# Latent attention on one core: ScalarE takes the exponential of the next unit before the copies of this unit's turned pieces

## The chip, the cores and the metric

One NeuronCore of a Trainium2 chip runs the whole layer. The metric is the device time of one execution in microseconds (us). The profile is of one execution of the same program. The engines are TensorE (PE; PEld is its weight load), VectorE (DVE), ScalarE (ACT), GpSimd (POOL) and SyncE (SP). Each engine runs its instructions in the order in which they are written for it, and waits for the others only at semaphores.

## The reference, cut to what matters

The layer is a hybrid decoder block on 1024 tokens of width 1024: latent attention (MLA) beside a chunkwise retention, then cross-attention to 256 memory tokens, then a gated convolution-MLP. The change touches the causal softmax attention of the eight MLA heads, with 64 + 32 query and key columns and 64 value columns:

```python
s = jnp.einsum('bhqd,bhkd->bhqk', q_blk, k).astype(jnp.float32) * scale
s = jnp.where(kpos[None, :] <= qpos[:, None], s, neg)
p = jax.nn.softmax(s, axis=-1).astype(v.dtype)
return jnp.einsum('bhqk,bhkd->bhqd', p, v)
```

Every product of the kernel is made of three matmuls, since each operand is held as a high and a low part (the high part is a rounded copy, the low part is the full value less the copy).

## The kernel before

Latent attention is worked in 64 **units**, eight for each of eight heads. A unit is a block of 128 queries, number i, with the keys of the blocks 0 to i, so it has (i + 1) x 128 columns. Within a head the blocks come in the order 1, 3, 2, 0, 5, 7, 6, 4 (`QORDER`). This text calls the places of a head r0 to r7, so r0 has 256 columns, r1 512, r2 384, r3 128, r4 768, r5 1024, r6 896 and r7 640. Units r0 to r3 have one **piece** of up to 512 columns, r4 to r7 have two.

What a unit w goes through:

- PE `m_scores(w)` (L824): the scores into PSUM banks 2 and 3, or 4 and 5. They are written two units ahead of the turning.
- DVE `m_max(w)` (L2138): the row maximum (L2143) and its negative times the scale (L2146), which raises `m_neg`.
- ACT `m_exp(w)` (L1444): it waits for `m_neg` and writes the exponentials of the whole row into `prow` (L1449), with the row sum.
- PE `m_turn(w)` (L845): it waits for `m_exp`, then transposes `prow` 128 columns at a time (L852) into bank 6 or 7, which the pieces take by turns. Piece q waits until the low part of piece q - 2 has been taken.
- ACT `m_pth(w)` (L1452): a rounded copy of each turned piece (`p0h` or `p1h`, the high part; the line shown by the profile is the helper's, L1178).
- DVE `m_ptl(w)` (L2149): the low part of each piece (`p0l` or `p1l`, L1829), which sets the bank free.
- PE `m_pv(g)` (L856): after four units (a half head) the products with the values (L873), 12 matmuls for the first half of a head and 24 for the second, then `ainv` turned into bank 0 (L886). ACT `m_sum(g)` copies that (`oT`), DVE `m_out(g)` multiplies (L2171).
- `aux(h + 1, n)`: in the units r2, r3, r4 and r6 PE makes a part of the next head's keys or queries in bank 0 (L547, L552, L553, or L818); ACT `aux_hi` copies it (`kbh`, `mqh`), DVE `aux_lo` takes the low part (`kbl`, `mql`). In the last head there is none; the output's high and low parts (`oth`, `otl`) are made there instead.

The order of each engine is written out by hand in a loop over the units, with nothing that reorders it. In iteration w the engines have:

- PE: `m_turn(w)`, `aux`, `m_scores(w + 2)`, and where w is a multiple of four `m_pv(w // 4 - 1)`.
- ACT: `m_sum` (where w % 4 is 1), `m_pth(w)`, `m_exp(w + 1)`, `aux_hi`.
- DVE: `m_out` (where w % 4 is 1), `m_ptl(w)`, `aux_lo`, `m_max(w + 2)`, then the reciprocal of the row sum, `m_inv(w + 1)` (L2162).

After the loop come the turning of x, the mixing product, and the rest of the layer, nearly all of it bound by PE. SP and POOL prepare weights for later stages meanwhile (`raw`, `wh`, `over_rings`); only the four slabs for the mixing product wait for PE's last use of the slot in this stage (L818).

Of the kernel before, what the change touches and what calls it, by code (L numbers as in the profile page):

```python
# [135 lines left out]
def build(nc, x, mem, pos, slabs, small, const, out):  # L136
# [23 lines left out]
    with ctx:  # L160
# [1015 lines left out]
        def _(act):  # L1176
# [243 lines left out]
            def aux_hi(h, n):  # L1420
                act.wait_ge(S["aux_t"], USE_OF["aux", h, n] + 1)
                b = n % 2
                if n < 2:
                    copy(kbh[0:NOPE, h % 2, half(b)], ps[0:NOPE, 0, :]).then_inc(S["aux_hi"], 1)
                else:
                    copy(mqh[0:QK, b, :], ps[0:QK, 0, :]).then_inc(S["aux_hi"], 1)

            def m_sum(g):

                h, b = divmod(g, 2)  # L1430
                r = slice(h % 2 * DV, (h % 2 + 1) * DV)
                act.wait_ge(S["aux_t"], USE_OF["sum", g] + 1)
                copy(oT[r, h // 2, half(b)], ps[r, 0, :]).then_inc(S["aux_hi"], 1)

            def o_hi(fb, b):
                act.wait_ge(S["aux_lo"], USE_OF["sum", 4 * fb + 2 + b] + 1)
                copy(oth[:, fb, half(b)], oT[:, fb, half(b)]).then_inc(S["o_hi"], 1)

            def s2(w):

                c = 2 + 2 * (w % 2)
                return ps[:, c:c + 2, :].rearrange("p a n -> p (a n)")

            def m_exp(w):  # L1444
                n = (UNITS[w][1] + 1) * P
                act.wait_ge(S["m_neg"], w + 1)
                if w >= 2:
                    act.wait_ge(S["m_ptt"], PIECE0[w - 1])
                act.activation(prow[:, w % 2, 0:n], s2(w)[:, 0:n], ACT.Exp, scale=QK ** -0.5,  # L1449
                               bias=aneg[:, 0, w % 4:w % 4 + 1], accum_out=asum[:, 0, w % 4:w % 4 + 1]).then_inc(S["m_exp"], 1)  # L1450

            def m_pth(w):  # L1452
                i, g = UNITS[w][1], w // CH
                at_least(act, S["m_pv"], g - 1)
                for n in range(i // CH + 1):
                    q = PIECE0[w] + n
                    c0, c1 = CH * n, min(CH * (n + 1), i + 1)
                    act.wait_ge(S["m_ptt"], q + 1)
                    copy((p1h if g % 2 else p0h)[:, c0:c1, i % CH * P:(i % CH + 1) * P],
                         ps[:, 6 + q % 2, 0:(c1 - c0) * P].rearrange("p (a n) -> p a n", n=P)).then_inc(  # L1460
                        S["m_pth"], 1)
# [3 lines left out]
            NW = len(UNITS)  # L1465
            m_exp(0)
            for w in range(NW):
                h, r = divmod(w, NT)
                if w > CH and w % CH == 1:
                    m_sum(w // CH - 1)  # L1470
                m_pth(w)
                if w + 1 < NW:
                    m_exp(w + 1)
                if r in AUX_AT and h + 1 < MH:
                    aux_hi(h + 1, AUX_AT[r])
                if h == MH - 1 and r < 4:
                    o_hi(r // 2, r % 2)
                if h == MH - 1 and r >= 6:
                    o_hi(2, r - 6)
# [1099 lines left out]
```

## Time and profile before

| | before |
|---|---|
| median of 3 runs | 1975.4 us (1971.09 to 1976.38) |
| profiled execution, its own time | 1980.84 us |
| its span in the profile | 1979.0 us |
| PE busy | 1855.0 us, 94% |
| PEld busy | 1536.0 us, 78% |
| DVE busy | 967.8 us, 49% |
| ACT busy | 668.3 us, 34% |
| POOL busy | 947.1 us, 48% |

Busy shares are averages over stages with different limits. The latent attention runs from 648.8 us, its first exponential, to about 860 us.

### The profile page before, as it was taken

To read this page: it belongs to the slowest core of one execution; us is meant where nothing else is said; L and a number is where in the kernel's file an instruction comes from. 1 tells how busy PE (TensorE), PEld (TensorE's weight loads), DVE (VectorE), ACT (ScalarE), POOL (GpSimd) and SP (SyncE) were. 2 spreads that over 40 slices of the span, in tenths; PEclk is the share of its full clock that TensorE was granted. 3 is DMA by queue.
4 is the path that set the end of the run, shared out by engine and by line. 5 is a ranking of instruction groups with operands and counts; after the bars stand their busy time and mean duration, and the time that the engine had idled before them with its cause. 6 is when DMAs were issued, how large, how long until landed. Compare 5 with 4: busy or idle time off the path is not lost.

```text
span 1979.0 us, 25491 instructions
## 1 busy us (share of the span) xinstructions
PE 1855.0 (94%) x8924; PEld 1536.0 (78%) x8924; DVE 967.8 (49%) x1531; ACT 668.3 (34%) x1161; POOL 947.1 (48%) x519
## 2 busy tenths in 40 slices
PE   7999999999997888879999989989999999699998
PEld 6788888888875777767878878768888888588887
DVE  4345454000007666637344553767777778732212
ACT  6322223110013555541132322544444444422212
POOL 5743333456644775204533213377777777533330
PEclk9999999999998899989999999999999999899999
DMA  6511111223314885034221114233333333453312
GB/s 243 202 33 33 32 42 43 85 96 95 95 54 164 308 314 193 22 132 166 96 91 59 61 57 160 80 102 128 116 127 118 120 128 111 171 192 126 107 54 85
DMA packets 69339, 229.55 MB, mean 116 GB/s; under 512 B 6544, under 2 KB 16912, under 8 KB 65936
## 3 DMA queue, kind: packets, MB, share of 16 engines
q1 hardware_dynamic: 48720, 159.31, 24.6%
q10 hardware_dynamic: 20544, 69.21, 9.3%
q8 instruction: 50, 0.82, 0.2%
q14 instruction: 25, 0.20, 0.0%
HBM read 168.73 MB, written 59.77 MB: 115 GB/s over the span
## 4 chain that ended last, share of the span: by engine, by line
PE 60%; issue 13%; POOL 12%; DVE 8%; ACT 5%; DMA 2%; POOLq 0%; ACTq 0%; SPq 0%; DVEq 0%
PE ps L547 17%; PE ps L552 17%; PE ps L553 17%; POOL wl L476 8%; PE ps L873 3%; POOL zB L483 2%; ACT prow L1449 1%; PE ps L852 1%; PE ps L1165 1%; PE ps L1167 1%; PE ps L1166 1%; DVE p1l L1829 1%; DVE t L1832 1%; DMA raw<-in_slabs 1%; DVE amax L2143 1%
## 5 line engine op out<-in xcount | busy, mean ns | idle before, releaser
L444 POOL TENSOR_SCALAR wh<-raw 128x1024 fp32r<-128x1024 f32 x76 | 210.7, 2772 | 599.2 <-PE ps L547 555.0
L547 PE MATMUL ps<-uh,wh 128*128 128x512 f32 (+1 forms) x576 | 229.3, 398 | 2.4 <-POOL wl L446 2.4
L552 PE MATMUL ps<-ul,wh 128*128 128x512 f32 (+1 forms) x576 | 226.1, 393 | 0.0
L553 PE MATMUL ps<-uh,wl 128*128 128x512 f32 (+1 forms) x576 | 226.0, 392 | 0.0
L446 POOL TENSOR_TENSOR wl<-raw,wh 128x1024 fp32r<-128x1024 f32 x76 | 181.7, 2391 | 6.4
L476 POOL TENSOR_TENSOR wl<-raw,wh 128x512 fp32r<-128x512 f32 x88 | 140.1, 1611 | 34.3 <-ACT wh L1178 34.3
L523 POOL TENSOR_TENSOR wl<-raw,wh 128x1024 fp32r<-128x1024 f32 x28 | 71.4, 2551 | 141.1 <-ACT wh L1178 141.1
L1832 DVE SCALAR_TENSOR_TENSOR ya<-zA,sm,ya 128x512 f32<-128x512 f32 x88 | 94.2, 1071 | 88.6 <-ACT ya L1687 81.4
L1832 DVE SCALAR_TENSOR_TENSOR yb<-zB,sm,yb 128x512 f32<-128x512 f32 x88 | 128.6, 1461 | 15.8 <-ACT yb L1687 9.6
L463 POOL TENSOR_TENSOR over_rings<-over_rings 128x512 f32<-128x512 f32 x88 | 112.9, 1284 | 45.8 <-DMA over_rings<-in_slabs 40.6
L1178 ACT ACTIVATE wh<-raw 128x512 fp32r<-128x512 f32 (+1 forms) x124 | 90.5, 748 | 115.8 <-PE ps L547 78.8
L547 PEld LDWEIGHTS ps<-uh,wh 128*128 128x128 f32 (+1 forms) x576 | 108.3, 188 | 25.8 <-POOL wl L446 2.6
L547 PE MATMUL ps<-fah,wh 128*128 128x512 f32 x288 | 113.4, 394 | 14.9 <-DVE fal L1829 14.4
L553 PEld LDWEIGHTS ps<-uh,wl 128*128 128x128 f32 (+1 forms) x576 | 107.9, 187 | 25.0
L552 PEld LDWEIGHTS ps<-ul,wh 128*128 128x128 f32 (+1 forms) x576 | 108.1, 188 | 23.1
L552 PE MATMUL ps<-fal,wh 128*128 128x512 f32 x288 | 113.0, 392 | 0.0
L553 PE MATMUL ps<-fah,wl 128*128 128x512 f32 x288 | 112.9, 392 | 0.0
L476 POOL TENSOR_TENSOR wl<-ssm,wh 128x512 fp32r<-128x512 f32 x44 | 66.5, 1513 | 75.3 <-ACT wh L1178 75.3
L2059 DVE TENSOR_TENSOR mxr<-ps,sig 128x512 f32<-128x512 f32 x16 | 11.1, 692 | 177.9 <-PE ps L553 177.9
L1063 PE MATMUL ps<-f0h,wh 128*128 128x512 f32 x176 | 70.3, 400 | 8.6 <-DVE u L2371 4.2
L547 PEld LDWEIGHTS ps<-fah,wh 128*128 128x128 f32 x288 | 54.7, 190 | 27.0 <-DVE fal L1829 14.8
L1065 PE MATMUL ps<-f0l,wh 128*128 128x512 f32 x176 | 70.1, 398 | 0.0
(426 smaller groups left out, 4835.9 us busy)
## 6 DMA issues: line engine op xcount, KB each, us to landing
raw<-in_slabs SPq DMA_DIRECT2D x134, 512.0 KB, 3.5
over_rings<-in_slabs SPq DMA_DIRECT2D x22, 1024.0 KB, 7.3
s_s<-over_rings SPq DMA_DIRECT2D x22, 1024.0 KB, 4.8
ssm<-s_s SPq DMA_DIRECT2D x22, 512.0 KB, 3.8
raw<-s_s SPq DMA_DIRECT2D x22, 512.0 KB, 4.6
s_f<-yb ACTq DMA_DIRECT2D x22, 512.0 KB, 2.6
fs<-s_f ACTq DMA_DIRECT2D x22, 512.0 KB, 3.4
a<-in_slabs SPq DMA_DIRECT2D x22, 256.0 KB, 2.6
```

Of the source, the lines that this page charges most:

```text
L444: pool.tensor_scalar(wh[:, j, :], raw[:, j % RAWS, :], 1.0, None, ALU.mult).then_inc(S["w_hi"], 1)
L446: pool.tensor_tensor(wl[:, j, :], raw[:, j % RAWS, :], wh[:, j, :].bitcast(f32), ALU.subtract).then_inc(S["w_ready"], 1)
L463: pool.tensor_tensor(o, p_, q_, op).then_inc(S["f_s"], 1)
L476: pool.tensor_tensor(wl[:, v // 2, half(v % 2)], src, wh[:, v // 2, half(v % 2)].bitcast(f32), ALU.subtract).then_inc(S["v_ready"], 1)
L523: pool.tensor_tensor(wl[:, n % SLOTS, :], raw[:, n % RAWS, :], wh[:, n % SLOTS, :].bitcast(f32), ALU.subtract).then_inc(S["w_ready"], 1)
L547: l = pe.matmul(o, lh, rh, start=start, stop=False)
L552: pe.matmul(o, lh, rl, start=False, stop=False)
L553: return pe.matmul(o, ll, rh, start=False, stop=stop)
L1063: l = pe.matmul(ps[:, bank, :], wh_, xh[:, k0 + k, :], start=not more and k == 0, stop=False, skip_group_check=True)
L1065: l = pe.matmul(ps[:, bank, :], wh_, xl[:, k0 + k, :], start=False, stop=False, skip_group_check=True)
L1178: return act.activation(o, i, ACT.Copy, **kw)
L1832: return dve.scalar_tensor_tensor(out=o, in0=a, scalar=s_, in1=b_, op0=op0, op1=op1)
```

## The change

In ACT's loop, `m_exp(w + 1)` moves from behind `m_pth(w)` to the head of iteration w, so ahead of `m_sum` and `m_pth(w)` both. Nothing else changes: the same instructions with the same waits, on all engines.

```diff
             m_exp(0)
             for w in range(NW):
                 h, r = divmod(w, NT)
+                if w + 1 < NW:
+                    m_exp(w + 1)
                 if w > CH and w % CH == 1:
                     m_sum(w // CH - 1)
                 m_pth(w)
-                if w + 1 < NW:
-                    m_exp(w + 1)
                 if r in AUX_AT and h + 1 < MH:
                     aux_hi(h + 1, AUX_AT[r])
```

## Rows read from the trace of the kernel before

**Rows 1.** Waits, 648 to 856 us: engine, tile, line <- releaser: us, times, longest.

```profile
POOL wh L444 <- PE ps L818: 35.9, 1, 35.9
PEld ps L852 <- ACT prow L1449: 35.2, 34, 1.8
PE ps L852 <- DVE p1l L1829: 18.7, 23, 1.6
ACT prow L1449 <- DVE aneg L2146: 13.1, 22, 0.9
```

**Rows 2.** Busy time of one whole head: stretch, length, engines, PEclk, DMA share, GB/s.

```profile
751.41:777.56 26.15, 22.46 (x138) 18.90 (x138) 17.15 (x44) 14.63 (x34) 15.62 (x11) 1.00 0.54 202
```

**Rows 3.** Timeline, ACT, exponentials: start, us, engine, line, out<-in, shape, [idle before].

```profile
751.41 0.47 ACT L1449 ACTIVATE prow<-ps,aneg 128x256 f32<-128x256 f32 x1 [0.18 <-DVE aneg L2146]
...
761.21 0.36 ACT L1449 ACTIVATE prow<-ps,aneg 128x128 f32<-128x128 f32 x1
...
767.48 1.12 ACT L1449 ACTIVATE prow<-ps,aneg 128x1024 f32<-128x1024 f32 x1 [0.75 <-DVE aneg L2146]
...
777.56 0.47 ACT L1449 ACTIVATE prow<-ps,aneg 128x256 f32<-128x256 f32 x1 [0.17 <-DVE aneg L2146]
```

**Rows 4.** Timeline, 758 to 766 us: ACT's copies, DVE's low parts and maxima.

```profile
758.97 0.60 ACT L1178 ACTIVATE p0h<-ps 128x512 fp32r<-128x512 f32 x1
...
759.77 0.69 DVE L1829 TENSOR_TENSOR p0l<-ps,p0h 128x512 fp32r<-128x512 f32 x1
760.38 0.28 DVE L2143 TENSOR_REDUCE amax<-ps 128x1 f32<-128x128 f32 x1
...
761.55 0.58 ACT L1178 ACTIVATE kbh<-ps 64x512 fp32r<-64x512 f32 x1
...
762.17 0.68 DVE L1829 TENSOR_TENSOR kbl<-ps,kbh 64x512 fp32r<-64x512 f32 x1 [0.26 <-ACT kbh L1178]
762.78 0.94 DVE L2143 TENSOR_REDUCE amax<-ps 128x1 f32<-128x768 f32 x1
762.80 0.28 ACT L1178 ACTIVATE p0h<-ps 128x128 fp32r<-128x128 f32 x1 [0.67 <-PE ps L852]
...
763.89 0.27 DVE L1829 TENSOR_TENSOR p0l<-ps,p0h 128x128 fp32r<-128x128 f32 x1
763.94 0.90 ACT L1449 ACTIVATE prow<-ps,aneg 128x768 f32<-128x768 f32 x1 [0.86 <-DVE aneg L2146]
...
766.05 1.21 DVE L2143 TENSOR_REDUCE amax<-ps 128x1 f32<-128x1024 f32 x1
```

**Rows 5.** Timeline: unit r0's turning, then the half head's sums behind the value products.

```profile
752.18 0.30 PE L852 MATMUL ps<-cn,prow 128*128 128x128 f32 x1 [0.89 <-DVE p1l L1829]
...
758.35 0.59 ACT L1178 ACTIVATE oT<-ps 64x512 f32<-64x512 f32 x1 [4.52 <-PE ps L886]
...
759.05 0.69 DVE L2171 TENSOR_TENSOR oT<-ps,oT 64x512 f32<-64x512 f32 x1 [4.79 <-ACT oT L1178]
```

**Rows 6.** Timeline: r0's exponential in the first, second and last head.

```profile
648.78 0.47 ACT L1449 ACTIVATE prow<-ps,aneg 128x256 f32<-128x256 f32 x1
...
672.65 0.47 ACT L1449 ACTIVATE prow<-ps,aneg 128x256 f32<-128x256 f32 x1 [0.23 <-DVE aneg L2146]
...
829.89 0.47 ACT L1449 ACTIVATE prow<-ps,aneg 128x256 f32<-128x256 f32 x1 [0.18 <-DVE aneg L2146]
```

**Rows 7.** Timeline, PE, end of the stage: the last turning, the last value products.

```profile
852.40 0.91 PE L852 MATMUL ps<-cn,prow 128*128 128x128 f32 x5 [1.58 <-DVE p1l L1829]
854.76 0.79 PE L873 MATMUL ps<-p1h,vrh 128*128 128x512 f32 x1 [1.46 <-DVE p1l L1829]
```

**Rows 8.** Busy time by stretch, columns as in rows 2, for the granted clock.

```profile
695.00:700.00 5.00, 3.44 (x26) 2.79 (x25) 4.03 (x12) 3.56 (x9) 4.31 (x4) 1.00 0.70 284
...
852.80:856.20 3.40, 1.94 (x7) 1.29 (x6) 2.18 (x4) 1.35 (x4) 0.00 (x0) 0.51 0.45 143
856.20:859.60 3.40, 3.40 (x9) 2.63 (x8) 0.00 (x0) 0.00 (x0) 0.00 (x0) 0.50 1.04 419
```

## The prediction

> **What bounds the kernel now.** I read the engine totals first: PE is busy for 94% of the span, so whatever lengthens PE's path lengthens the program. Then the busy time by stretch, for one whole head of the latent attention, from one exponential of 256 columns to the next [rows 2, 3]. A head takes 777.56 - 751.41 = 26.15 us, in which PE is busy for 22.46, DVE for 17.15 and ACT for 14.63. The three heads that I looked at beside it are the same to 0.02 us. So no engine is full: PE has 3.7 us of holes in a head, and the head is set by PE's work and by the hand-overs around it. Third, the waits of the stage [rows 1]. PE's weight load waits 35.2 us in all for the exponentials, in 34 of the 64 units, and PE waits 18.7 us for DVE's low parts, which free the banks of the turned pieces. ACT's exponential waits only 13.1 us for DVE's maximum. The loop that matters now is exponential, turning, copy, next exponential: ACT holds exponential w + 1 back until PE has turned unit w and the copies are done.
>
> **What the change removes.** That loop. Exponential w + 1 needs only its own maximum and the free half of `prow`, so the turning of w + 1 could follow that of w at once. What it is worth at most: all of PE's holes, 3.7 us in a head, some 29 us in eight.
>
> **What it adds.** ACT's order is strict, so the copies of w now stand behind exponential w + 1, and exponential w + 1 stands at a semaphore until `m_neg` of w + 1 is there. Queued behind that wait are `m_sum`, the copies of w and `aux_hi`. Who waits for those: DVE's low parts of w, PE's second next piece (it needs the bank), PE's aux products. The decisive one is DVE. Its order is low parts of w, `aux_lo`, then the maximum of w + 2. So there is a new closed loop with no PE in it:
>
> exponential w + 1 -> copy of w -> low parts of w -> (aux low part) -> maximum of w + 2 -> exponential w + 2.
>
> Before, the copies of w came first, so DVE worked on w while ACT did exponential w + 1; now these two go one after the other. Every unit must take at least one turn of this loop.
>
> **The durations.** All from rows, between the narrowest and the widest by a straight line, and to two digits. Exponential E: 0.36 us for 128 columns, 1.12 for 1024 [rows 3]: 0.47, 0.58, 0.69, 0.79, 0.90, 1.01 between. Copy C: 0.28 for 128, 0.60 for 512 [rows 4]. Low part L: 0.27 and 0.69, so 0.41 and 0.55 between; the first of two pieces counts 0.61, since 759.77 to 760.38 is start to start. Maximum M: 0.28 for 128, 1.21 for 1024, 0.133 for each 128 more. Handovers [rows 4]: ACT starts the next instruction 0.02 before an exponential's end (761.21 + 0.36 against 761.55). ACT to DVE 0.04 (762.13 to 762.17). DVE starts the next 0.08 before a low part's end. From a maximum's end over its negative to the exponential 0.22 (762.78 + 0.94 = 763.72 against 763.94). So one turn is E + C + L + M + 0.16, and 0.61 more where there is an aux low part (762.17 to 762.78).
>
> **One head of the changed kernel**, exponential start to exponential start, the unit r in brackets:
>
> - (r0) to (r3), where the value products stand in PE's way: turning r0 waits for the bank that the low part of r7's first piece frees, at 0.45 + 0.60 + 0.04 + 0.69 + 0.04 = 1.82 us after exponential r0. From turning r0 to the maximum of r3 PE, ACT and DVE do what they do now, 752.18 to 760.38 = 8.20 us, with `m_sum` at 758.35 and `m_out` at 759.05 between [rows 4, 5]. Then 0.28 + 0.22. Sum 10.52. Before it is 761.21 - 751.41 = 9.80 [rows 3].
> - (r3) to (r4): 0.36 + 0.49 + 0.55 + 0.94 + 0.16 + 0.61 = 3.11.
> - (r4) to (r5): here `aux_hi` is the late one: 0.88 + 0.20 for the short copy, 0.62 from `aux_hi` to `aux_lo` (761.55 to 762.17), 0.61, then 1.21 + 0.22. Sum 3.74. Before, 767.48 - 763.94 = 3.54.
> - (r5) to (r6): 1.12 + 0.60 + 0.61 + 0.41 + 1.08 + 0.16 + 0.61 = 4.59.
> - (r6) to (r7): `m_sum` is in front of the copies: 0.99 + 0.70 + 0.72 to the first low part (758.35 to 759.05 to 759.77), 0.61 + 0.61, then 0.81 + 0.22. Sum 4.66.
> - (r7) to the next r0: 0.79 + 0.60 + 0.61 + 0.55 + 0.41 + 0.16 + 0.61 = 3.73.
>
> Together 30.35 us, against 26.15: **4.20 us more in a head**. The gain at PE's waits is real, but it is not on the new path; PE's holes grow to about 7.9 us.
>
> **The whole stage.** Six full heads (second to seventh): 6 x 4.20 = 25.2. First head, now 672.65 - 648.78 = 23.87 [rows 6]: no value products ahead of it, and PE on the low clock for a part of it, so PE's scores bind down to r4; I put exponential r4 at about 9.5 us, then 3.74 + 4.59 + 4.66 + 3.73 = 16.72, sum 26.2, so 2.3 more. This is my loosest term, 0 to 4. Last head, from 829.89 to the last value products at 854.76, 24.87 [rows 6, 7]: without the aux steps 10.52 + 2.50 + 2.82 + 3.98 + 4.66, then 0.77 + 0.60 + 0.04 + 0.69 + 0.04 = 2.14 to the last turning and 2.36 from there to the products (852.40 to 854.76). Sum 28.98, so 4.1 more. Total 25.2 + 2.3 + 4.1 = **31.6 us**.
>
> **What lies beside it, at no cost.** The only transfers in ACT's queue here are issued after the loop and shift with it. POOL's split of the slabs for the mixing product is let go by PE's L818 in the seventh head [rows 1], with a whole head, which gets longer too, as cover; that cover gone, it would cost up to the 20 us of four slabs. The work of later stages is PE's, and starts later by what the stage is longer.
>
> **Size of the unknowns.** No row shows an exponential that is followed by its predecessor's copies. The nearest are the handovers above, five in a turn; 0.05 us either way on each makes 0.25 x 6 x 8 = 12 us in the extreme, and I take a third of that, 4 us. Below: where a step of the loop is hidden behind PE's work the sum is too high; the first four units, where PE rules, may not pay their 0.7 us in each head, which takes off 6.
>
> **The clock.** At the end of the stage PE stood 1.58 and 1.46 us with little between [rows 7], and the granted clock fell to 0.50 (1.2 GHz) until 859.6 [rows 8]; over those 6.8 us PE was busy for 5.3, so half of that, 2.7 us, was lost. From 695 to 700 us, with 3.44 us busy of 5, it stayed at 1.00 (2.4 GHz). In the changed kernel each head has two holes of about 2 us around the turnings of r7 and r0, with short work between, which lies nearer to the first case. The Trainium skill, "TensorE: Matmul & The Clock Gate", section "HAM oscillation", puts such falls down to idle gaps longer than any that I find here; by that rule the clock would hold and the time would be that of the forecast. The trace speaks against resting on it, since the clock fell with no gap over 1.58 us.
>
> **The rivals.**
>
> 1. The clock falls in each head too. The work behind it, the long value products, is on the path. 2.7 us in seven heads is 19: 1975.4 + 31.6 + 19 = 2026, with falls in half of the heads 2016. For: the thin stretch. Against: between the two cases read there is no row. Chance 0.20, for over 2015.
> 2. The loop is partly hidden, and only the units with two pieces pay, half the sum: 1991. Against: ACT's and DVE's orders leave nowhere to hide. Chance 0.05.
> 3. Faster: PE's waits for the exponentials go and the new loop does not bind. It would do so from the point at which a turn of the loop is shorter than PE's work for a unit, 22.46 / 8 = 2.8 us. Half of PE's holes gone would be 8 x 1.85 = 15 us, so 1960. For: the turns behind r7 (0.47 + 0.60 + 0.61 + 0.27 + 0.68 + 0.16 = 2.79) and behind r0 are that short. Against: the other turns are 3.1 to 4.7. Chance 0.03.
> 4. No effect, since the old and the new loop are equally long: 1975. Against: the sum by rows. Chance 0.02.
>
> **The numbers.** The forecast, chance 0.70: the profiled execution would go from 1980.84 to 2012.4; the median lies 5.4 us under that execution, so 1975.4 + 31.6 = 2007.0. Within a case ± 7 us by the unknowns above. The range reaches down to 1999 and up to 2021, into rival 1. Faster by over 0.3% (about what a measurement of this kernel can tell from no change, 6 us) 0.03, within it 0.02, slower 0.95.
>
> **What would show it.** Right: in the profile after, the waits of ACT's exponential for `aneg` are far above 13 us, as ACT now stands there in nearly each unit, with DVE's maximum ending just before; DVE waits for `p0h` and `p1h` in nearly each unit; PE's wait for the exponentials falls and its wait for the low parts rises; a head takes 30 us, PE's busy time in it stays 22.5. Wrong: a head of 26 us or less; a granted clock under 1.00 within the heads (rival 1); a maximum of w + 2 that ends before exponential w + 1 does, which would break the loop that the sum stands on.

## The result

The changed kernel is slower. Median of four runs 2023.88 us (2022.36 to 2024.73), before 1975.89 us (four runs, 1971.09 to 1982.45); ratio 1.0241, 95% interval 1.0222 to 1.0259. So 48 us more, where 31.6 were forecast: 2023.88 lies above the forecast 2007.0 and above the range, which ended at 2021. The direction and the closed loop were right; the clock, which fell in each head behind the first, was left out of the sum.

The page of the changed kernel: the span, the engines' line, and two lines of part 5 that belong to the stage (line, engine, op, shapes, count, then busy time, mean of one, idle time ahead and who ended it):

```profile
span 2022.5 us, 25491 instructions
...
PE 1876.4 (93%) x8924; PEld 1552.5 (77%) x8924; DVE 966.7 (48%) x1531; ACT 666.4 (33%) x1161; POOL 947.7 (47%) x519
...
L852 PE MATMUL ps<-cn,prow 128*128 128x128 f32 x288 | 50.6, 308 | 34.0 <-DVE p1l L1829 31.8
L1449 ACT ACTIVATE prow<-ps,aneg 128x256 f32<-128x256 f32 (+3 forms) x64 | 47.4, 741 | 103.5 <-DVE aneg L2146 103.5
```

DVE and ACT are as busy as before; PE is busy for 21.4 us more with the same matmuls, which points to a lower clock for some of them. The waits of the stage, from 648 to 905 us:

```profile
ACT prow L1449 <- DVE aneg L2146: 102.7, 62, 2.6
POOL wh L444 <- PE ps L818: 75.0, 1, 75.0
DVE oT L2171 <- ACT oT L1178: 55.4, 15, 6.8
...
PE ps L852 <- DVE p1l L1829: 31.8, 23, 2.6
DVE p1l L1829 <- ACT p1h L1178: 31.6, 24, 1.7
DVE p0l L1829 <- ACT p0h L1178: 23.3, 24, 1.2
...
PEld ps L852 <- ACT prow L1449: 2.8, 3, 1.6
```

Against [rows 1]: PE's wait for the exponentials, 35.2 us, is gone (2.8), and in its place ACT stands 102.7 us at the maxima, in 62 of 64 units, where it stood 13.1 in 22. DVE now stands at ACT's copies in 48 cases, 54.9 us. PE's wait at the low parts went from 18.7 to 31.8. POOL waits longer for L818, 75.0 us, but its work is not late for anybody: from the last value products to the end of the program the changed kernel takes 1124.7 us (897.84 to 2022.5), against 1124.2 before (854.76 to 1979.0).

The loop itself, the end of the fifth head, ACT's and DVE's timeline put together (against [rows 3, 4]):

```profile
797.32 0.81 DVE L2143 TENSOR_REDUCE amax<-ps 128x1 f32<-128x640 f32 x1
...
798.35 0.80 ACT L1449 ACTIVATE prow<-ps,aneg 128x640 f32<-128x640 f32 x1 [1.98 <-DVE aneg L2146]
...
799.13 0.97 ACT L1178 ACTIVATE p1h<-ps 128x512 fp32r<-128x512 f32 x2
...
799.76 1.16 DVE L1829 TENSOR_TENSOR p1l<-ps,p1h 128x512 fp32r<-128x512 f32 x2 [1.37 <-ACT p1h L1178]
800.83 0.68 DVE L1829 TENSOR_TENSOR mql<-ps,mqh 96x512 fp32r<-96x512 f32 x1
801.42 0.41 DVE L2143 TENSOR_REDUCE amax<-ps 128x1 f32<-128x256 f32 x1
...
802.06 0.47 ACT L1449 ACTIVATE prow<-ps,aneg 128x256 f32<-128x256 f32 x1 [1.48 <-DVE aneg L2146]
```

Read it in order: the maximum of r7 at 797.32, exponential r7 at 798.35, the copies of r6 behind it at 799.13, DVE starts on their low parts 0.63 us later, then the aux low part (`mql`), the maximum of the next r0, and only then the next exponential, at 802.06. That is 3.71 us for one unit; the sum had 3.73.

Busy time and clock of a whole head (the fifth), to be read beside [rows 2], and of stretches around the holes in PE (length, PE, PEld, DVE, ACT, POOL, PEclk, DMA share, GB/s):

```profile
769.12:802.06 32.94, 26.43 (x136) 22.35 (x136) 17.18 (x43) 14.29 (x35) 9.18 (x4) 0.83 0.10 32
```

```profile
763.10:766.50 3.40, 1.96 (x15) 1.67 (x15) 2.28 (x6) 1.44 (x4) 0.00 (x0) 1.00 0.44 110
766.50:769.90 3.40, 1.55 (x9) 1.10 (x9) 2.30 (x6) 1.92 (x6) 1.87 (x1) 1.00 0.60 242
769.90:773.30 3.40, 2.26 (x8) 2.19 (x9) 2.01 (x6) 1.50 (x5) 3.32 (x3) 0.53 0.00 0
773.30:776.70 3.40, 3.40 (x10) 2.63 (x9) 0.81 (x4) 0.67 (x2) 3.32 (x2) 0.50 0.46 154
```

A head that took 26.15 us takes 32.94. PE was busy for 3.51 of the 6.8 us from 763.1 to 769.9, its granted clock fell to 0.50 (1.2 GHz), and the value products ran into that. PE's timeline there, the turnings of r6, r7 and r0 and the first value products:

```profile
764.01 1.05 PE L852 MATMUL ps<-cn,prow 128*128 128x128 f32 x7 [1.86 <-DVE p1l L1829]
...
767.65 0.74 PE L852 MATMUL ps<-cn,prow 128*128 128x128 f32 x5 [1.69 <-DVE p1l L1829]
...
771.04 0.66 PE L852 MATMUL ps<-cn,prow 128*128 128x128 f32 x2 [1.84 <-DVE p1l L1829]
...
772.68 0.63 PE L873 MATMUL ps<-p1h,vrh 128*128 128x512 f32 x1
773.10 0.63 PE L873 MATMUL ps<-p1l,vrh 128*128 128x512 f32 x1
```

The products start 0.43 us apart, where 0.23 is their distance at full clock (769.08 to 769.31 in the run e1_fill below).

**Step by step.** Exponential start to exponential start, in us, for the fifth head (for e1 the fourth, ahead of which the clock had not fallen), each read from the timeline. The sum's first figure is for r0 to r3 together.

| | r0-r1 | r1-r2 | r2-r3 | r3-r4 | r4-r5 | r5-r6 | r6-r7 | r7-r0 | head |
|---|---|---|---|---|---|---|---|---|---|
| before | 1.65 | 6.40 | 1.75 | 2.73 | 3.54 | 4.68 | 2.77 | 2.63 | 26.15 |
| the prediction's sum | 10.52 | | | 3.11 | 3.74 | 4.59 | 4.66 | 3.73 | 30.35 |
| changed | 2.80 | 2.19 | 8.35 | 3.11 | 3.70 | 4.56 | 4.52 | 3.71 | 32.94 |
| e1_fill | 2.80 | 2.20 | 5.51 | 3.11 | 3.71 | 4.57 | 4.78 | 3.71 | 30.39 |
| e2_first | 1.64 | 2.19 | 5.64 | 3.11 | 3.70 | 4.68 | 2.78 | 2.63 | 26.37 |
| e3_second | 2.96 | 9.08 | 1.75 | 2.72 | 3.55 | 4.56 | 4.51 | 3.71 | 32.84 |
| e6_more_after | 2.99 | 2.39 | 7.91 | 3.30 | 3.90 | 4.76 | 4.71 | 3.90 | 33.86 |
| e7_more_before | 1.84 | 6.21 | 1.74 | 2.93 | 3.74 | 4.68 | 2.77 | 2.83 | 26.74 |
| e8_max_first | 2.79 | 2.20 | 6.04 | 2.51 | 4.51 | 3.96 | 4.90 | 3.11 | 30.02 |
| e4_r1 | 1.65 | 1.16 | 6.68 | 2.75 | 3.53 | 4.69 | 2.77 | 2.63 | 25.86 |
| e5_both | 1.68 | 1.00 | 6.24 | 2.84 | 3.54 | 4.03 | 4.03 | 2.34 | 25.70 |
| e9_r6_early | 1.69 | 0.99 | 6.24 | 2.85 | 3.54 | 2.18 | 5.08 | 2.34 | 24.91 |

### The profile page after: what moved, and what is told of

Read it like the earlier page. It is cut to its first block, busy times and chain, and to the rows that moved or that the text cites. A ratio compares the mean times of both kernels' runs of the same rounds, so it can differ in the third digit from the quotient of the medians.

```text
span 2022.5 us, 25491 instructions
## 1 busy us (share of the span) xinstructions
PE 1876.4 (93%) x8924; PEld 1552.5 (77%) x8924; DVE 966.7 (48%) x1531; ACT 666.4 (33%) x1161; POOL 947.7 (47%) x519
## 4 chain that ended last, share of the span: by engine, by line
PE 58%; issue 14%; POOL 11%; DVE 10%; ACT 4%; DMA 2%; POOLq 0%; ACTq 0%; SPq 0%; DVEq 0%
PE ps L547 17%; PE ps L552 16%; PE ps L553 16%; POOL wl L476 8%; PE ps L873 2%; POOL zB L483 2%; DVE amax L2143 2%; DVE p1l L1829 1%; PE ps L1165 1%; PE ps L1167 1%; PE ps L1166 1%; DVE t L1832 1%; ACT p1h L1178 1%; ACT prow L1449 1%; PE ps L852 1%
## 5 line engine op out<-in xcount | busy, mean ns | idle before, releaser
L553 PEld LDWEIGHTS ps<-uh,wl 128*128 128x128 f32 (+1 forms) x576 | 107.9, 187 | 24.9
L852 PE MATMUL ps<-cn,prow 128*128 128x128 f32 x288 | 50.6, 308 | 34.0 <-DVE p1l L1829 31.8
L1449 ACT ACTIVATE prow<-ps,aneg 128x256 f32<-128x256 f32 (+3 forms) x64 | 47.4, 741 | 103.5 <-DVE aneg L2146 103.5
```

The source lines that it names most:

```text
L553: return pe.matmul(o, ll, rh, start=False, stop=stop)
L852: l = pe.transpose(ps[:, 6 + q % 2, (c % CH) * P:(c % CH + 1) * P], prow[:, w % 2, c * P:(c + 1) * P], ident)
```

## The experiments

The theory was A, the closed loop exponential, copy, low part, maximum, exponential, plus PE's clock. B is the rival theory, a different one in each run.

**e1_fill: is the rest the clock?** The changed kernel with work put into PE's holes.

```diff
                 if w + 2 < NW:
                     m_scores(w + 2)
+                if r >= 6 and h + 1 < MH:
+                    for _ in range(7):
+                        pe.matmul(ps[:, 1, :], ident_r[:, :], vrh[:, 0, :], start=True, stop=True)
                 if w and w % CH == 0:
                     m_pv(w // CH - 1)
```

> The changed kernel, with 7 more matmuls of 128x512 on PE in each of the iterations r6 and r7 of the first seven heads, written into bank 1 while it is free (their result is overwritten; nothing of the computation is left out). They take 7 x 0.23 = 1.6 us of the two holes of about 2 us in front of the turnings of r7 and of the next r0. Theory A, that what the sum missed is the clock alone: the granted clock is 1.00 within the heads, the step from exponential r2 to r3 falls from 7.2 to 8.6 us in the changed kernel to 5.5, a head takes 30.4 us, and the time goes from 2024 to about 2008. Theory B, that the value products are slow for another reason (the copies and low parts of two units beside them, or the banks): the step stays over 7 us and the time at 2024 or above, by up to 7 x 2 x 1.6 = 22 us if the holes do not hold the new matmuls.

Median 2011.47 us, ratio to before 1.0177 (1.0152 to 1.0202), so some 12 us less than the changed kernel with 98 matmuls more. Two of its heads by busy time and clock:

```profile
734.81:765.20 30.39, 25.95 (x146) 21.84 (x145) 17.18 (x43) 14.43 (x34) 20.49 (x16) 0.94 0.75 279
765.20:796.26 31.06, 26.85 (x162) 22.50 (x161) 17.19 (x43) 14.33 (x35) 10.28 (x4) 1.00 0.25 81
```

In the fourth, sixth and eighth heads the step r2 to r3 is 5.51 or 5.52 us, and the fourth takes 30.39 in all; the sum had 30.35. In the second, third, fifth and seventh it is 6.35 to 6.45 us. The clock is full at the value products there too, but it had fallen for about 3.4 us at the end of the head before (the fourth head's 0.94). The turning of r6 and what follows it took longer, the filling behind it started 1.83 us after exponential r7 (763.32) instead of 0.40 as in the third head, and PE came late to the value products, with turning r0 at 767.99, 2.79 us after its exponential instead of 1.93. So theory A holds for the value products, and B falls: the same instructions beside them leave them fast once PE is kept busy. The expectation that the clock stays at 1.00 within the heads was missed. The four falls that remained, beside the one at the end of the stage, stand at the hole ahead of turning r6 (1.59, 1.87, 1.86 and 1.87 us), which the filling does not cover, and 0.9 us in each of four heads is about what 2011 lies above 2008.

**e2_first and e3_second: which units pay?** ACT's loop with `early = r in (0, 1, 2, 3)`, and with `(4, 5, 6, 7)`:

```diff
+                if early and w + 1 < NW:
+                    m_exp(w + 1)
                 if w > CH and w % CH == 1:
                     m_sum(w // CH - 1)
                 m_pth(w)
-                if w + 1 < NW:
+                if not early and w + 1 < NW:
                     m_exp(w + 1)
```

> The change in the iterations r0 to r3 alone (one piece each), the old order in r4 to r7. Theory A, the closed loop through DVE, adds it up step by step: r0 to r1 stays 1.65, r1 to r2 goes to 2.2, r2 to r3 (value products, clock 1.00) 5.2 to 5.5, r3 to r4 3.1, the others stay: a head 26.1 to 26.4 us, the time +2 to +4 us against before. Theory B, that a mere change of ACT's order costs everywhere: half of the change's 48 us, so +24.

> The change in the iterations r4 to r7 alone (two pieces each, the long maxima). Theory A: r6 to r7 4.5, r7 to r0 3.7, r0 to r1 2.8, against 2.8, 2.6 and 1.65 before; with them PE has its two holes and the clock falls as in the changed kernel, so the value products take 7 to 8.5 us. A head is 29.9 us by the loop and 2.3 more by the clock, the time +45 us against before, nearly all of the change. Theory B: +24.

e2_first: ratio 1.0014 (0.9999 to 1.0030), some 3 us, which is not clear of no change, and 26.37 us for a head. e3_second: ratio 1.0235 (1.0210 to 1.0259), 46 us, 32.03 to 32.91 us for the second to the seventh head. Nearly the whole cost sits in r4 to r7: in the first half of a head the wait for the value products swallows what the order costs (2.19 + 5.64 against 6.40 + 1.75), and 0.38 us more from r3 to r4 and 0.16 from r4 to r5 are left. The two versions do not cost half of the change's 48 us each, so theory B falls. One head of e2_first, the fourth, had a fall of the clock all the same, with the step r2 to r3 at 8.49; here it is behind the third:

```profile
697.27:723.93 26.66, 22.50 (x138) 18.83 (x138) 17.15 (x44) 14.56 (x34) 20.88 (x18) 1.00 0.91 324
723.93:753.29 29.36, 25.48 (x138) 21.19 (x138) 17.17 (x44) 14.56 (x35) 22.78 (x18) 0.88 0.87 315
```

**e6_more_after and e7_more_before: does the loop run through DVE?** The same short instruction in both kernels:

```diff
                 at_least(dve, S["m_exp"], w - 1)
+                dve.tensor_reduce(amax[:, 1, w % 4:w % 4 + 1], ps[:, c, 0:P], AX.X, ALU.max)
                 dve.tensor_reduce(amax[:, 0, w % 4:w % 4 + 1],
```

> The changed kernel with one more short maximum (128 columns, about 0.2 us from start to start, its result not used) ahead of each unit's maximum on DVE. Theory A, a closed loop through DVE: every step but the one of the value products (r2 to r3, where there is slack) grows by the full 0.2 us: r0 to r1 3.0, r1 to r2 2.4, r3 to r4 3.3, r4 to r5 3.9, r5 to r6 4.8, r6 to r7 4.7, r7 to r0 3.9. Theory B, that PE or ACT sets the steps: they stay as in the changed kernel.

> The kernel before with the same short maximum added. Theory A: DVE is in no closed loop there, and only the steps behind whose exponential ACT waited for the maximum grow by 0.2 us (r0 to r1, r3 to r4, r4 to r5, r7 to r0), the others (r1 to r2 and r2 to r3 together, r5 to r6, r6 to r7) stay within 0.05. Theory B: as much as in the changed kernel, seven of eight steps.

DVE's timeline in e6_more_after shows the price of it, 842.55 to 842.75, 0.20 us:

```profile
842.55 0.28 DVE L2143 TENSOR_REDUCE amax<-ps 128x1 f32<-128x128 f32 x1
842.75 0.41 DVE L2144 TENSOR_REDUCE amax<-ps 128x1 f32<-128x256 f32 x1
```

Both came as theory A had it. In the changed kernel seven of eight steps are 0.19 to 0.20 us longer. In the kernel before only four are (r0, r3, r4, r7), and r1 to r2 is 0.19 shorter, since the value products end it anyway. The program took 2033.70 us and 1982.26 us, one run each, so only the steps are evidence.

**e8_max_first: and through the aux low part?** The changed kernel, DVE's order:

```diff
+                if w + 2 < NW:
+                    m_max(w + 2)
                 if r in AUX_AT and h + 1 < MH:
                     aux_lo(h + 1, AUX_AT[r])
-                if w + 2 < NW:
-                    m_max(w + 2)
```

> The changed kernel with DVE's order turned in one place: the maximum of w + 2 ahead of the aux low part, in the iterations r2, r3, r4 and r6 that have one. Theory A: the 0.6 us of the aux low part leave the loop at the unit that has them, so r3 to r4 goes from 3.1 to 2.5 and r5 to r6 from 4.6 to 4.0 and r7 to r0 from 3.7 to 3.2, but the aux product then holds PE's next scores back, and r4 to r5 goes to 4.5 and r6 to r7 to 4.8: a head 0.8 us shorter in all. Theory B, that the loop does not go through DVE: nothing moves, or the heads get longer by PE's later aux products alone.

In the second, third and fifth heads all five steps moved about as expected, in the fifth to 2.51, 4.51, 3.96, 4.90 and 3.11; 2021.66 us in one run. The loop lost 0.6 us in three steps and got two thirds of it back in two, where PE's aux product and scores come later. In other heads of this run the clock fell: the step r2 to r3 took up to 8.46 us, r4 to r5 5.0 to 5.5 in three heads, so its time says little.

**e4_r1: is there a place where the change costs nothing?** `early = r in (1,)`, rest as in e2_first.

> The change in the iteration r1 alone, in which ACT stands 4.5 us at the sums of the value products: exponential r2 moves into that stand. Theory A: it costs nothing there, PE finds r2 ready after turning r1, a head takes 25.8 us instead of 26.15, so -0.35 x 7 = -2.5 us: 1973. Rival: the low parts of r1 and maximum r3 are what PE and ACT wait for, so no difference, 26.15.

The step r1 to r2 fell from 6.40 to 1.16 and r2 to r3 rose from 1.75 to 6.68; the undisturbed heads take 25.83 to 25.86 us, 0.3 less, as theory A had it. In the program it is not to be seen: ratio 0.9992 (0.9977 to 1.0008), from 5 us less to 2 us more, which neither shows nor excludes the 2.5 us expected. Two heads of the profiled execution had a fall of the clock and took 27.4.

**e5_both, e9_r6_early, e10_end_fill: a version that uses what is learnt.** Exponentials ahead only where ACT would stand anyway, and DVE's maxima ahead only where no low part is waited for. e9_r6_early, on the kernel before:

```diff
 # ScalarE
+                if r in (0, 1, 5) and w + 1 < NW:
+                    m_exp(w + 1)
                 if w > CH and w % CH == 1:
                     m_sum(w // CH - 1)
                 m_pth(w)
-                if w + 1 < NW:
+                if r not in (0, 1, 5) and w + 1 < NW:
                     m_exp(w + 1)
 # VectorE
+                if r == 0 and w + 2 < NW:
+                    m_max(w + 2)
                 if w > CH and w % CH == 1:
                     m_out(w // CH - 1)
+                if r == 1 and w + 2 < NW:
+                    m_max(w + 2)
                 m_ptl(w)
+                if r >= 4 and w + 2 < NW:
+                    m_max(w + 2)
                 if r in AUX_AT and h + 1 < MH:
                     aux_lo(h + 1, AUX_AT[r])
-                if w + 2 < NW:
+                if r in (2, 3) and w + 2 < NW:
                     m_max(w + 2)
```

e5_both is the same, except that in r5 the exponential stands between `m_sum` and `m_pth`.

> The order of before with single exponentials moved where they close no loop: ACT takes exponential r2 ahead of the sums in iteration r1, r1 and r6 ahead of the copies in r0 and r5 (behind the sums, where there are any), and DVE takes the next-but-one maximum first in r0, ahead of the low parts in r1, and ahead of the aux low part in r4 and r6. Added up by the same durations as the prediction's, a head takes 24.5 to 24.8 us instead of 26.15: steps 1.7, 1.0, 5.9, 3.0, 3.6, 2.2, 4.9, 2.3 from r0 on. Theory A: 7 heads x 1.4 = -10 us, 1966 to 1968, less what a fall of the clock takes, 1 to 3 us in a head where it falls. Rival, that any exponential taken ahead of the copies costs: 26.2 us or more in a head, no gain.

> The kernel e5_both with exponential r6 ahead of the sums in iteration r5 too; there it stood behind them, at 758.70 against sums at 758.21, and gained nothing. By the durations of the sum it starts 2.2 us after exponential r5 instead of 4.0, the steps r5 to r6 and r6 to r7 together 7.1 us instead of 8.1, a head 24.5 to 24.9 us against 26.15 before. Theory A: 7 heads x 1.3 = -9 us against before, 1967. Rival, that PE's value products or the low parts set these two steps: 25.7 us in a head, as in e5_both.

e5_both missed: ratio 0.9985 (0.9974 to 0.9997), 3 us instead of 10, a head 25.7 to 26.0 (its profiled execution, 1963.86 us, is the fastest of 13 and not typical; the median is 1975.12). Its trace names the place: exponential r6 started right behind the sums, which wait for PE, though its maximum had been there for 2 us:

```profile
756.66 0.15 DVE L2150 TENSOR_SCALAR aneg<-amax 128x1 f32<-128x1 f32 x1
...
758.21 0.59 ACT L1178 ACTIVATE oT<-ps 64x512 f32<-64x512 f32 x1 [1.85 <-PE ps L886]
758.70 0.99 ACT L1449 ACTIVATE prow<-ps,aneg 128x896 f32<-128x896 f32 x1
```

Moved ahead of the sums (e9_r6_early), it comes 2.18 us after exponential r5 instead of 4.03:

```profile
759.71 1.12 ACT L1449 ACTIVATE prow<-ps,aneg 128x1024 f32<-128x1024 f32 x1 [0.75 <-DVE aneg L2148]
761.89 1.01 ACT L1449 ACTIVATE prow<-ps,aneg 128x896 f32<-128x896 f32 x1 [0.49 <-DVE aneg L2148]
763.25 0.59 ACT L1178 ACTIVATE oT<-ps 64x512 f32<-64x512 f32 x1 [0.26 <-PE ps L886]
```

A head takes 24.9 to 25.2 us, a little more than the 24.5 to 24.9 expected, and the program 1967.71 us, ratio 0.9952 (0.9933 to 0.9971): faster than both kernels, by 9.5 us against before. Apart from e4_r1, with exponential r2 alone, no run moves exponentials without DVE's maxima, and none moves these maxima alone, so how much of the gain each of them gives is not shown. Last, e9_r6_early with filling at the end:

```diff
+                if w >= NW - 2:
+                    pe.wait_ge(S["aux_lo"], USE_OF["sum", 2 * MH - 2] + 1)
+                    for _ in range(6):
+                        pe.matmul(ps[:, 1, :], ident_r[:, :], vrh[:, 0, :], start=True, stop=True)
             m_pv(2 * MH - 1)
```

> e9_r6_early with 6 more matmuls of 128x512 in bank 1 after each of the last two turnings, in the holes of 1.6 and 1.5 us ahead of the last value products (overwritten, nothing left out). They take 6 x 0.23 = 1.4 us of each. Theory A, that the low clock at the end of the stage costs half of PE's busy time in it: the clock stays at 1.00 up to the last value products, which take 4.6 us instead of 6.9, so 2 to 2.7 us less than e9_r6_early. Rival: the clock falls all the same, or the holes are too short, and it is 0 to 1 us more.

Inconclusive: 1967.26 us, ratio to before 0.9958 (0.9942 to 0.9974), the same as without. The last value products did run at full clock, 4.8 us (839.19 to 843.95) against 6.4 (844.51 to 850.89 in e9_r6_early). But in the profiled execution a fall came earlier in the same head (steps r4 to r5 and r5 to r6 2.91 and 3.29 us against 2.56 and 2.40), and the first head was longer (22.39 against 21.57), so the stage as a whole took 203.3 us in both, from the first exponential to the last turning of the sums. What remains open is whether the fill pays in the mean over executions.

## Why the prediction was wrong in its size

- **What bounds.** Right: what lengthened the stage lengthened the program. From the first exponential to the last value products it is 205.98 us before (648.78 to 854.76) and 253.15 in the changed kernel (644.69 to 897.84), 47.2 more. The medians are 48 apart. The spans of the two profiled executions are only 43.5 apart, since the stage began 4.1 us earlier in that of the changed kernel; in all the runs it begins between 639 and 649 us.
- **The loop and its durations.** Right to 0.15 us in every step from r3 on: 3.11, 3.74, 4.59, 4.66, 3.73 summed, 3.11, 3.70, 4.56, 4.52 or 4.79, 3.71 measured. e6 and e8 show that the loop runs through DVE's maximum and the aux low part, e2 and e3 that it costs in r4 to r7.
- **The first head**, the loosest term: 2.3 us more, measured 26.30 - 23.87 = 2.4.
- **The step that failed: r0 to r3, 10.52 us in a head.** It was taken from the kernel before with its full clock, as 8.20 us from turning r0 to the maximum of r3. Its last part, r2 to r3, is 5.52 if the measured 2.80 and 2.20 are taken from the sum's 10.52. It took 7.16 to 8.64 us in the seven heads that have value products there, 54.8 us together against 38.6: **16.2 us short**, the whole of the miss (47.2 - 31.6 = 15.6). The granted clock of 0.50 and the 0.43 us between the products, in place of 0.23, show that this is the clock, and so does e1_fill, where the same step is 5.51 us in three heads and at most 6.45 in the others. With it went the sign that PE's busy time in a head stays at 22.5 us: it was 26.43.
- **Where the choice was made.** The holes that the loop opens were in the prediction, as two of about 2 us (there are up to three, of 1.6 to 1.9 us, ahead of the turnings of r6, r7 and r0), and their likeness to the end of the stage [rows 7, 8] too. Rival 1 had the price nearly right, 2.7 us in seven heads, 19 us, 2026; measured it is 16.2 / 7 = 2.3. But it got a chance of 0.20, and the range stopped inside it. The rows that were there, a fall after holes of 1.6 us with little between, spoke for it; against it stood only that no row lay between the two cases. The rule of the Trainium skill that was weighed ("TensorE: Matmul & The Clock Gate", section "HAM oscillation"), that idle gaps longer than these bring the clock down, would have kept it up; the measurement decides against it here, since it fell in each head behind the first, and no gap in the full heads was over 1.87 us (2.60 in the last).
- **Rivals 2, 3 and 4** are out: each step paid in full; PE's wait for the exponentials did go (35.2 to 2.8 us), but apart from r5 to r6 (0.1 us) no step got shorter by it except those inside the wait for the value products.

## What to carry to other kernels

When an order is changed on an in-order engine, write down the closed loop that it makes (here exponential, copy, low part, maximum) and add up one turn for each kind of unit: the sums agreed with the trace to 0.15 us. Then ask what the holes in PE do to its clock, and price the long matmul run behind them at both levels. An instruction goes ahead of a wait only where its own input is there before that wait ends. Moving exponentials ahead everywhere cost 48 us; moving three of eight, together with some of DVE's maxima, gained 9.5.

## What the hardware showed that was not expected

The clock of TensorE fell without a long pause: from 763 to 770 us in the changed kernel PE was busy for about half of the time, with no hole over 1.9 us, and then ran at 0.50 (1.2 GHz) for 6.8 us, though the value products gave it full work from 772.68 on. The same falls came now and then in kernels whose holes are shorter (one head of e2_first, two of e4_r1, neither with a hole of 1 us there, and one of e7_more_before, with 1.09), which makes up 1.5 to 3 us in a head where it happens. On the other side, the third head of e8_max_first had a hole of 2.02 us (717.08, ahead of PE's aux product) and kept its full clock to the end; it fell at about 733.5, behind a hole of 1.69 us:

```profile
703.32:732.95 29.63, 22.56 (x141) 18.80 (x139) 17.16 (x43) 14.53 (x34) 21.86 (x18) 1.00 0.90 328
```

And in e4_r1 the same work came before a fall and before none. Here are the 3.4 us ahead of the sixth and of the eighth head, each followed by a stretch at its start:

```profile
767.13:770.53 3.40, 2.62 (x19) 1.94 (x16) 2.44 (x9) 2.90 (x7) 3.32 (x2) 1.00 0.00 0
771.00:774.40 3.40, 3.10 (x10) 2.84 (x11) 2.39 (x9) 1.60 (x6) 3.32 (x3) 0.53 0.51 154
821.90:825.30 3.40, 2.61 (x19) 1.93 (x16) 2.45 (x9) 2.89 (x7) 2.91 (x2) 1.00 0.26 104
825.80:829.20 3.40, 3.13 (x16) 2.79 (x17) 2.95 (x10) 2.29 (x7) 0.00 (x0) 1.00 0.45 154
```

So neither the longest hole nor PE's busy time ahead tells by itself, in these runs, whether the clock falls; what decides it stays open. The spread of one kernel from execution to execution goes with the clock: of the kernel before, the fastest took 1967.90 us at a mean granted clock of 0.981, the slowest 1982.64 us at 0.971.
